# Two-layer hybrid backbone: first expert tile by a selection product, next layer's inputs requested during the expert passes

## The reference

```
mod = silu(cond) @ w_mod + b_mod            # six vectors: sh1, sc1, g1, sh2, sc2, g2
u = h * (1 + sc1) + sh1
m = mix(u)       # u @ w_in (2432 columns); then RWKV-7 in both directions | attention with rotary |
                 # pooling; then @ w_out
h = layer_norm(ALPHA * h + g1 * m, ln1_g, ln1_b)
u = h * (1 + sc2) + sh2
f = hier_moe(u)  # pick one of 4 groups, two of its 4 experts; 16 experts, D_EXPERT = 256
h = layer_norm(ALPHA * h + g2 * f, ln2_g, ln2_b)
# hier_moe: y = sum over a token's 2 experts of gate * (silu(u @ w1[e]) * (u @ w3[e])) @ w2[e]
```

## Time and profile before

| | |
|---|---|
| timed runs (3) | 1189.32, 1192.55, 1193.77 us; median 1192.55 |
| the profiled execution: its own time | 1185.78 us |
| its span, first to last instruction | 1184.0 us |
| its mean granted TensorE clock | 0.926 of full speed |
| VectorE, ScalarE, GpSimd busy | 500.2, 316.4, 95.9 us |
| moved by DMA | 225.20 MB, 190 GB/s in the mean |

### The profile page before, as it was taken

One profiled execution on the slowest core, in us unless ns is written; L12 is line 12 of the kernel. 1 busy time (PEld: TensorE's weight loads), 2 busy tenths in 40 slices (PEclk: granted clock), 3 DMA queues, 4 the chain that ended last, 5 costly groups with the idle time before them and its releaser, 6 DMA issues. The chain is left out here.

```text
span 1184.0 us, 28495 instructions
## 1 busy us (share of the span) xinstructions
PE 990.0 (84%) x12516; PEld 600.0 (51%) x12516; DVE 500.2 (42%) x1366; ACT 316.4 (27%) x731; POOL 95.9 (8%) x130
## 2 busy tenths in 40 slices
PE   3999999779797988999847999878888997999930
PEld 3866656667675463333316655567676463333310
DVE  0103855352625452433225249646555443433126
ACT  1231116333331131112114320454532041112111
POOL 1200000000100001211130000000010001111110
PEclk9899998888899998999977999889989999999975
DMA  9877625252628454999848233100011564899851
GB/s 351 303 217 271 244 92 232 74 187 103 256 76 250 142 224 150 319 372 368 312 175 234 99 108 106 39 2 4 3 46 60 191 256 141 306 371 365 294 208 55
DMA packets 144856, 225.20 MB, mean 190 GB/s; under 512 B 20803, under 2 KB 98864, under 8 KB 143904
## 3 DMA queue, kind: packets, MB, share of 16 engines
q1 hardware_dynamic: 131712, 185.61, 46.5%
q0 software_dynamic: 10880, 30.39, 7.0%
q10 hardware_dynamic: 2128, 7.21, 1.6%
HBM read 217.77 MB, written 21.14 MB: 202 GB/s over the span
## 5 line engine op out<-in xcount | busy, mean ns | idle before, releaser
L1491 ACT ACTIVATE region<-bank 128x512 f32<-128x512 f32 (+3 forms) x322 | 155.0, 512 | 247.5 <-PE bank L1410 73.8
L1384 PE MATMUL bank<-region 128*32 128x512 f32 x1152 | 174.1, 610 | 11.7 <-issue 8.9
L1384 PEld LDWEIGHTS bank<-region 128*32 128x32 f32 x1152 | 49.1, 112 | 117.4 <-issue 117.4
L1122 PE MATMUL bank<-u,ring 128*128 128x384 f32 x320 | 106.5, 488 | 0.0
L1288 PE MATMUL bank<-ring,u 128*128 128x512 f32 x192 | 87.6, 613 | 8.1 <-DVE u L2241 5.9
L1410 PE MATMUL bank<-ring,region 128*32 128x512 f32 x768 | 87.3, 595 | 1.4 <-ACT region L1491 1.4
L1122 PEld LDWEIGHTS bank<-u,ring 128*128 128x128 f32 x320 | 59.9, 190 | 40.5 <-issue 1.4
L2159 DVE COPY_PREDICATED region<-lev,bank 128x256 f32<-128x256 uint8 x90 | 34.1, 442 | 106.4 <-PE bank L945 106.4
L2374 DVE TENSOR_TENSOR region<-region,bank 128x256 f32<-128x256 f32 x24 | 10.1, 421 | 142.3 <-ACT region L1803 111.9
L1558 ACT ACTIVATE region<-bank 128x384 f32<-128x384 f32 x50 | 23.7, 492 | 168.4 <-PE bank L1122 96.7
L1288 PEld LDWEIGHTS bank<-ring,u 128*128 128x128 f32 x192 | 37.2, 197 | 53.6 <-issue 43.5
(11 more groups left out here) (292 smaller groups left out, 1489.3 us busy)
## 6 DMA issues: line engine op xcount, KB each, us to landing
ring<-in_w_mod SPq DMA_DIRECT2D x48, 1024.0 KB
region<-in_moe_w SPq DMA_DIRECT2D x48, 1024.0 KB
ring<-in_moe_w SPq DMA_DIRECT2D x48, 1024.0 KB
ring<-in_w_in SPq DMA_DIRECT2D x20, 768.0 KB
region<-y_rows SPq DMA_DIRECT2D x6, 1024.0 KB, 10.7
region<-g_rows POOLq DMA_DIRECT2D x4, 1024.0 KB, 5.6
ring<-in_w_in SPq DMA_DIRECT2D x12, 256.0 KB
ring<-in_w_out SPq DMA_DIRECT2D x4, 768.0 KB
```

What stands on the lines that cost most here:

```text
L1122: last = pe.matmul(dst[:, 0:T], w[:, c, tc(m)], u[:, c, :], start=(c == 0), stop=(c == KT - 1))
L1384: last = pe.matmul(bank[p % 2][cols, :], xs[:, p % 2, c, cols], of[(p * P + CTILE * q) // CAP][:, c, :], start=(c == 0), stop=(c == KT - 1))
L1491: return act.activation(dst, src, ACT.Copy)
```

## The change

1. TensorE no longer runs `turn_in(0)` on gathered rows. VectorE writes, before `pick(0)`, the fp32 selection matrix of tile 0 into `over_m` (six compares, `first_up`), and `select_first` multiplies the tokens that are in SBUF (`u_tok`) with it: 2 halves of 4 chunks by 3 token tiles, straight into the layout that `turn_in` gave. The order is `select_first(0)`, `rows_of(0)`, `select_first(1)`, `rows_of(1)`; the six fillers and `gather(0)` are gone. `gather(3)` needs no wait for its buffer.
2. The next layer's `in` items 0 and 1 (`EARLY_IN`) stand in `ORDER` right after the experts, before the overflow items and before `fy`; overflow items use slots 3 to 5 only.
3. The next layer's small inputs are requested by GpSimd in six parts, after `scatter(p-1)` of the passes p = 3 to 8. `small_inputs(l, part)` holds the twelve DMAs of before, two a part: 0 is `rw_w2`, `rw_a2`; 1 `rw_g2`, `pool_w`; 2 the router weights; 3 the router biases; 4 `cache_k`, `cache_v`; 5 the states.
4. The `ln2` rows of layer 0 are requested after the next layer's `u` is written; those of the last layer in its last pass, before `scatter(10)`, into a ring slot (`rows_end`) that `w13` of the last expert has left; `result_rows` reads them there.
5. ScalarE runs one small root before it waits for `fy`, so that its table is loaded there.

```diff
+EARLY_IN = 2
...
-        ORDER += [("in", _l, _i)]
+        ORDER += [("in", _l, _i)] if _l == 0 or _i >= EARLY_IN else []
...
+    ORDER += [("in", _l + 1, i) for i in range(EARLY_IN)] if _l + 1 < DEPTH else []
     for _o in range(OVERS):
         ORDER += [("over13", _l, _o), ("over2", _l, _o)]
...
+        elif kind in ("over13", "over2"):
+            slot, over = RING + over % EXTRA, over + 1
         else:
-            slot, turn = (RING + turn) % (RING + EXTRA), turn + 1
+            slot, turn, over = (RING + turn) % (RING + EXTRA), turn + 1, 0
...
+        rows_end = ring[:, SLOT_OF[PLACE["w13", DEPTH - 1, NE - 1]], 0:2 * D].rearrange("p (k n) -> p k n", k=2)
...
+            def small_inputs(l, part):
...
             for l in range(DEPTH):
-                if l > 0:
-                    pool.wait_ge(route_mm, l)
-                    pool.wait_ge(si_mm, l)
...
+                if l == 0:
+                    for part in range(SMALL_PARTS):
+                        small_inputs(0, part)
                 u_ready(pool, 2 * l, NT - 1)
                 pool.dma_start(bands, a["bands"]).then_inc(bands_in, 16)
...
                 def gather(p):
-                    if p >= GATHERED:
+                    if p > GATHERED:
                         pool.wait_ge(xt_mm, 2 * (ROUNDS * l + p - GATHERED + 1))
...
-                gather(0)
                 gather(1)
                 for p in range(PASSES):
                     if p + 2 < PASSES:
                         gather(p + 2)
+                    if p == PASSES - 1 and l + 1 == DEPTH:
+                        pool.wait_ge(hid_mm, ROUNDS * l + PASSES)
+                        for k, name in enumerate(("ln2_g", "ln2_b")):
+                            pool.dma_start(rows_end[:, k, :], a[name][l:l + 1].broadcast_to([P, D])).then_inc(n2_in, 16)
                     if p >= 1:
                         scatter(p - 1)
+                    if l + 1 < DEPTH and 3 <= p < 3 + SMALL_PARTS:
+                        pool.wait_ge(route_mm, l + 1)
+                        pool.wait_ge(si_mm, l + 1)
+                        small_inputs(l + 1, p - 3)
...
                 scatter(PASSES - 1)
-                for b in range(2):
-                    pool.wait_ge(ys_out[b], 16 * PASSES // 2 * (l + 1))
-                pool.wait_ge(zo_up, NT * HALVES * OVERS * (l + 1))
-                for k, name in enumerate(("ln2_g", "ln2_b")):
-                    pool.dma_start(rows_a[:, k, :], a[name][l:l + 1].broadcast_to([P, D])).then_inc(n2_in, 16)
+                if l + 1 < DEPTH:
+                    u_ready(pool, 2 * (l + 1), NT - 1)
+                    for k, name in enumerate(("ln2_g", "ln2_b")):
+                        pool.dma_start(rows_a[:, k, :], a[name][l:l + 1].broadcast_to([P, D])).then_inc(n2_in, 16)
...
+                def select_first(half):
+                    n = ROUNDS * l
+                    if half == 0:
+                        pe.wait_ge(first_up, l + 1)
+                        pe.wait_ge(utok_cp, 2 * NT * (l + 1))
+                        pe.wait_ge(xs_cp, 2 * n)
+                    for c in range(4 * half, 4 * half + 4):
+                        for t in range(NT):
+                            last = pe.matmul(bank[2 + half][:, tc(c % 4)], u_tok[:, t, tc(c)], over_m[:, t, :],
+                                             start=(t == 0), stop=(t == NT - 1))
+                    last.then_inc(xt_mm, 1)
+
+                select_first(0)
                 rows_of(0)
-                keep_running(bank[6], 3)
+                select_first(1)
                 rows_of(1)
-                keep_running(bank[6], 3)
-                turn_in(0)
...
+                act.activation(table_use[:, 0:1], eps[:, 2:3], ACT.Sqrt)
                 act.wait_ge(gate_up, l + 1)
...
+                for t in range(NT):
+                    for e, at, n, first_rank in parts_of(0):
+                        last = ts(over_m[:, t, at:at + n], slots[:, first_rank:first_rank + n], slot_code[:, t, e:e + 1],
+                                  None, ALU.is_equal)
+                last.then_inc(first_up, 1)
                 for p in range(2):
                     pick(l, p)
                     rows_of(l, p)
```

More of the change, by code:

```diff
@@ L90, in place_items @@
 def place_items():
-    slot_of, prev_of, last, turn = [], [], [-1] * (RING + EXTRA), 0
+    slot_of, prev_of, last, turn, over = [], [], [-1] * (RING + EXTRA), 0, 0
     for n, (kind, _, _) in enumerate(ORDER):
@@ L110 @@
 SMALL = 12
+SMALL_PARTS = 6
 def item_dmas(item):
@@ L236, in build @@
         norm_rs = sb("norm_rs", [P, NT])
+        table_use = sb("table_use", [P, 1])
         u = sb("u", [P, KT, T])
@@ L437, in build @@
         gate_up, over_up, zo_up = sem("gate_up"), sem("over_up"), sem("zo_up")
+        first_up = sem("first_up")
         x_init = sem("x_init")
@@ L534, in used, with landed_gather @@
             return (hid_mm if kind == "over13" else down_mm), ROUNDS * l + PASSES + i + 1
+        def landed_gather(l, p):
+            slot = p % GATHERED
+            per_layer = PASSES // GATHERED - (1 if slot == 0 else 0)
+            return 16 * (per_layer * l + p // GATHERED + (0 if slot == 0 else 1))
         def slot_view(n):
@@ L665, in _ @@
             pool.wait_ge(mod_mm, 3)
-            for l in range(DEPTH):
-                if l > 0:
-                    pool.wait_ge(route_mm, l)
-                    pool.wait_ge(si_mm, l)
[L670 to L684, removed]
@@ new lines, in small_inputs @@
+            def small_inputs(l, part):
+                if part == 0:
+                    pool.dma_start(lora_w2[:, :], a["rw_w2"][l].rearrange("d r c -> (d r) c")).then_inc(small_in, 16)
+                    pool.dma_start(lora_a2[:, :], a["rw_a2"][l].rearrange("d r c -> (d r) c")).then_inc(small_in, 16)
+                elif part == 1:
+                    pool.dma_start(lora_g2[:, :], a["rw_g2"][l]).then_inc(small_in, 16)
+                    pool.dma_start(pool_w[:, :, :],
+                                   a["pool_w"][l].rearrange("(t g) c d -> t (g c) d", t=2).rearrange("t p d -> p t d")
+                                   ).then_inc(small_in, 16)
+                elif part == 2:
+                    pool.dma_start(route_w[:, :, 0:NG], a["rt_grp_w"][l].rearrange("(c p) n -> p c n", p=P)).then_inc(small_in, 16)
+                    pool.dma_start(route_w[:, :, NG:20], a["rt_exp_w"][l].rearrange("(c p) n -> p c n", p=P)).then_inc(small_in, 16)
+                elif part == 3:
+                    pool.dma_start(route_b[:, 0:NG], a["rt_grp_b"][l:l + 1, :]).then_inc(small_in, 16)
+                    pool.dma_start(route_b[:, NG:20], a["rt_exp_b"][l:l + 1, :]).then_inc(small_in, 16)
+                elif part == 4:
+                    pool.dma_start(ctx_k[:, :], a["cache_k"][0, l].rearrange("t h c -> t (h c)")).then_inc(small_in, 16)
+                    pool.dma_start(ctx_v[:, :], a["cache_v"][0, l].rearrange("t h c -> t (h c)")).then_inc(small_in, 16)
+                else:
+                    for d in range(2):
+                        pool.dma_start(state_nat[rows64(d), :, :].rearrange("p j n -> p (j n)").rearrange("p (h k) -> p h k", h=AH),
+                                       a["state_rwkv"][0, l, d].rearrange("h v k -> v h k")).then_inc(small_in, 16)
@@ L1364, in turn_in @@
                     n = ROUNDS * l + p
-                    pe.wait_ge(xg_in[p % GATHERED], 16 * (PASSES // GATHERED * l + p // GATHERED + 1))
+                    pe.wait_ge(xg_in[p % GATHERED], landed_gather(l, p))
                     pe.wait_ge(xs_cp, 2 * n)
@@ L1944, in result_rows @@
                 dve.wait_ge(mv_up, NT * (k - 1) + t + 1)
-                link(stt(h[:, t, :], h[:, t, :], norm_mv[:, t, 0:1], rows_a[:, 0, :], ALU.subtract, ALU.mult))
+                link(stt(h[:, t, :], h[:, t, :], norm_mv[:, t, 0:1], rows_end[:, 0, :], ALU.subtract, ALU.mult))
                 dve.wait_ge(ln_rt, NT * (k - 1) + t + 1)
                 link(dve.reciprocal(norm_rs[:, t:t + 1], norm_rs[:, t:t + 1]))
-                stt(h[:, t, :], h[:, t, :], norm_rs[:, t:t + 1], rows_a[:, 1, :], ALU.mult, ALU.add).then_inc(y_up_s, 1)
+                stt(h[:, t, :], h[:, t, :], norm_rs[:, t:t + 1], rows_end[:, 1, :], ALU.mult, ALU.add).then_inc(y_up_s, 1)
             def mixed_in(l, t):
```

## The result

The changed kernel takes 1175.05 us (median of 4 runs, 1170.21 to 1177.45) against 1190.93 before (4 runs, one more than the forecast had); the ratio is 0.9851, 95% interval 0.9816 to 0.9885. Its profiled execution took 1175.39 us with a span of 1173.6.

What follows compares the result with a forecast made beforehand. TensorE was busy 990.0 of 1184.0 us, its passes at TensorE's and DMA's limits at once. Terms -6.9 - 1.5 + 4.3 + 1.1 - 1.6 - 4.3 = -8.9 us gave a median of 1183.6, range 1177 to 1191.

Steps and rivals of the forecast that it cites:

- layer 1's stalls "unchanged": Expert passes of layer 1: TensorE's stalls in hidden stay as they were, 0 us of difference.
- 373 GB/s as the ceiling of the weight stream: Expert passes: DMA moves 373 GB/s at share 1.07, the rate used to price extra bytes.
- Rival 2: Layer change: clock stays up, 2.6 us more, with free small inputs 4.3 more; sum -15.8, 1176.8; chance 0.09.
- 2.6 us of clock: first_piece at the layer change: 2.6 us more gained if TensorE's clock stays up after the shorter idleness.
- Selection: Start of the expert passes: selection products replace gathered rows, -6.9 us in layer 0 and -1.5 in layer 1.
- Small inputs, +4.3: Passes 3 to 8 of layer 0: loads delay weights, 2.3 us for bytes and 2.0 for small pieces.
- Early items: Layer change: early in items 0 and 1 bring the front's first product -4.3 us, last scatter +1.6.
- rival 1: Passes bound by the weight stream, DMA takes it back: sum -4.9, about -2 at low clock, 1190.5; chance 0.22.
- `fy`, -1.6 at the end: End of the run: fy load without ln2 rows beside it takes 4.6 us instead of 6.2, -1.6.
- Root ahead: nothing: Behind fy at the layer change: loading the root's table ahead gains nothing, since turn_tile(0) waits for keep_running.
- `ln2` rows later: nothing: Layer 0's ln2 rows: VectorE's scaling comes 8 us later within 22.94 us of idleness, costing nothing.
- Late gathers (rival 3): Six passes: gathers wait behind small inputs on GpSimd's queue, 3.5 us each; sum +7.8, 1200; chance 0.09.

Runs made afterwards that it cites:

- moved-back pair: The changed kernel with table_use allocated behind all other tiles, 0.9937 to the kernel before, beside the kernel before with only the selection product added, 0.9904.

## Why the prediction was wrong

The direction was right and the size was not. The step that failed is the one that named layer 1's stalls "unchanged" and took 373 GB/s as the ceiling of the weight stream for both kernels: the rate depends on where the buffers start, and the diff moved them by 32 bytes through a tile that I read only as "one small root". In the traces this is worth 6.8 us of the passes (144.1 and 138.8 against 146.2 and 143.5 moved back), 4.7 of them in layer 1; at the timed ratios (0.984 or 0.9851 against 0.9937) it is 10 to 12 us, with intervals of some 4 us on each. Either is about the whole missing 7 or more. I had put the stalls down to bytes, which is right, but never asked how fast a byte lands. Rival 2 gave nearly the measured time, for another reason: neither its free small inputs nor its 2.6 us of clock came (1.0 did). Had it been the forecast, it would have been right by luck.

With the buffers moved back the change came out near the forecast (0.9937, 7.5 us, against 8.9), but partly because errors cancel. From the rank product on, that trace is 10.5 us shorter than the first of the kernel before. Its passes of layer 0 are 3.6 us longer, near my 4.3, but 2.7 of that is low clock; the first `fy` of layer 0 comes 2.4 later, where I had 1.1; the selection gives 1.2 more than I had; and the end is 1.3 shorter, near my 1.6, for a reason that does not hold (below).

Step by step:
- *Selection.* Right, in both layers: halves of 2.9 us, `hidden(0)` 8.7 us after the rank product (forecast 9.3; the six compares took 1.07 us, not 1.43). Layer 0 gained 7.5, of which 2.8 are the clock. I took it that layer 1 has no clock to win; in the second trace of the kernel before it had.
- *Small inputs, +4.3.* Right in kind: 4.8 us of passes, but only 3.0 of it is the weights coming later, where I had 4.3. The small pieces are 1.1 of that, not 2.0, and the bytes 1.9, not 2.3. The moved-back pair agrees: there the stalls and the low clock up to the second stall of layer 0 are 8.5 us, against 5.4 with the selection alone, 3.1 more. The other 1.7 of the 4.8 are not DMA time. Behind the 3.33 us stall of the changed kernel the granted clock was partly low, and the next `hidden` took 8.8 us in place of 7.07 (pass 9 of layer 0; clock 0.81):

```profile
563.70:572.50 8.80, 8.77 (x65) 2.92 (x66) 0.00 (x0) 0.00 (x0) 0.51 (x1) 0.81 1.06 372
```

The length of the stall does not decide this. In the kernel before the clock stayed up behind 3.20 us in layer 0, and was partly low behind 2.56 in layer 1; both came back in its second trace (3.41 and 2.47 us):

```profile
565.84 7.07 PE L1384 MATMUL bank<-region 128*32 128x512 f32 x64 [3.20 <-issue]
...
1096.12 8.77 PE L1384 MATMUL bank<-region 128*32 128x512 f32 x64 [2.56 <-issue]
```

The stalls of layer 0 are 5.0 us before and after, so the +1.5 in the balance is this clock. The faster stream gave back what the small inputs cost: one column of padding alone took 3.1 us off these stalls.

- *Early items.* The cost was under-sized: +2.5 at the scatter in the two first traces, 3.7 against the kernel without them; I had +1.6. The upper bound of the whole step was also added up wrong: a scatter of 7.0 us is 3.1 more than 3.9, and with a slow `fy` the bound is +3.1, not +2.6, so rival 1 should read -4.4. The reason given for the gain was wrong: -3.6 us came, but from the other loads being gone, not from the items being early.
- *`fy`, -1.6 at the end.* Not there. The first `fy` of layer 1 took 5.7 us, 6.3 before, and between 4.9 and 6.4 over the traces, with and without `ln2` rows beside it (5.0 in the kernel before, run again). A term from a single pair of rows, within their scatter. The chain's row after, to the earlier trace rows:

```profile
1132.25 5.61 DMA region<-y_rows
```

- *Root ahead: nothing.* Right, and shown. *`ln2` rows later: nothing.* Right: VectorE waits 6.81 us for them and still idles 16.03 before the front needs it, to the earlier trace rows:

```profile
653.72 3.75 DVE L2011 TENSOR_TENSOR h<-h,region 128x1024 f32<-128x1024 f32 x3 [6.81 <-DMA region<-in_ln_b]
...
677.29 1.08 DVE L2034 TENSOR_SCALAR region<-region,par 128x384 f32<-128x384 f32 x3 [16.03 <-ACT region L1601]
```

- *Late gathers (rival 3).* Did not come: gathers landed in 7.3 us at most, and no product of TensorE in the passes waited for one.

## What to carry to other kernels

When a diff adds, drops or resizes an on-chip tile, work out what it does to the start of every DMA buffer allocated behind it; here large rows wanted a multiple of 256 bytes, and one unused tile made the old kernel 0.7% faster. Before crediting a gain to a moved load, take the move out alone: here the wait had gone because its neighbours had, and the early load itself only delayed the transfer on the path. Where transfers are the limit, what is put "under" them is paid: the small inputs made weights 3.0 us late in passes 3 to 8, and nothing that could be seen in passes 9 and 10 (138.2 us of passes, as with none), behind the last large request.

## What the hardware showed that I had not expected

- At a DMA share of 1.06 to 1.07, in the same 24 us of the passes, the same 1 KB and 4 KB rows came at 368 to 375 GB/s with `region` 32 bytes short of a multiple of 256 or 64 bytes past one, and at 380 to 388 at a multiple of 256. In the stretch that answers to `ring`, aligning `ring` took it from 379 or 382 to 396.
- Waiting for weights can cost more than the wait. In layer 1 of the kernel before, `hidden` took 1.7 us more behind 2.56 us of standing, with the clock partly at its lower level, and with one column of padding 1.7 more behind 1.91. Behind 3.20 us in layer 0 of the kernel before it took nothing more, at full clock. What decides it stays open.
